# Five changes along one transformer step: the root step ahead of the weight splits, one modulation row on TensorE, shorter routing, the last index mask among the query norms, five row loads ahead of the barrier

## What is computed

```python
mod = jnp.matmul(jax.nn.silu(c), ada_w[l]) + ada_b[l]
sh1, sc1, gt1, sh2, sc2, gt2 = [m[:, None, :] for m in jnp.split(mod, 6, axis=-1)]
h = rmsnorm(x, norm1_g[l]) * (1.0 + sc1) + sh1
proj = jnp.matmul(h, w_in[l])
...
out_fox = forgetting_attention(fq, fk, fv, log_f)       # softmax with a decay
out_dsa = dsa_attention(dq, dk, dv, iq, ik, iw)         # keys chosen by an index score
...
x = x + gt1 * jnp.matmul(merged, w_out[l])
h2 = rmsnorm(x, norm2_g[l]) * (1.0 + sc2) + sh2
y = hierarchical_moe(h2, ...)
x = x + gt2 * y
```

## Time and profile before

| what | value |
|---|---|
| time of the runs, median of three | 3393.41 us (3392.14 to 3396.78) |
| time of the profiled execution | 3398.27 us |
| its span in the trace | 3396.5 us |
| TensorE busy with matmuls | 3149.5 us, 93% of the span |
| VectorE busy | 2199.0 us, 65% |
| ScalarE busy | 1329.4 us, 39% |
| GpSimd busy | 988.8 us, 29% |
| moved by the DMA engines | 446.19 MB, mean 131 GB/s |

### The profile page before, as it was taken

The page is one execution under the profiler, slowest core; times in us unless marked ns, Lnnn a source line. Parts: engine busy times, 40 slices in busy tenths (PEclk is TensorE's granted clock), DMA queues, the critical chain, the costliest instruction groups (busy, mean ns, idle before and its releaser), DMA issues. The chain is left out here.

```text
span 3396.5 us, 44909 instructions
## 1 busy us (share of the span) xinstructions
PE 3149.5 (93%) x15126; PEld 2510.4 (74%) x15126; DVE 2199.0 (65%) x2729; ACT 1329.4 (39%) x1768; POOL 988.8 (29%) x489
## 2 busy tenths in 40 slices
PE   5989989888789499999969999999999999999998
PEld 4658866565578478888857888888778888888877
DVE  7788875677544799999966776633565145245366
ACT  3345423566512388888853156201311000000142
POOL 2223322000043011111102443345234444444433
PEclk8999989899999799999989999999999999999999
DMA  6312221231151599999982122133221111111312
GB/s 241 81 50 87 75 56 55 65 120 43 44 169 69 208 377 380 378 380 383 380 314 97 50 82 91 50 121 90 83 85 44 49 49 49 50 44 49 111 38 69
DMA packets 351447, 446.19 MB, mean 131 GB/s; under 512 B 32943, under 2 KB 235613, under 8 KB 351333
## 3 DMA queue, kind: packets, MB, share of 16 engines
q1 hardware_dynamic: 336612, 410.08, 35.6%
q10 hardware_dynamic: 5360, 17.83, 1.6%
q0 software_dynamic: 9360, 16.80, 1.3%
HBM read 397.40 MB, written 58.75 MB: 134 GB/s over the span
## 5 line engine op out<-in xcount | busy, mean ns | idle before, releaser
L424 PE MATMUL acc<-Ah,whi 128*128 128x512 f32 x2208 | 875.8, 397 | 24.8 <-ACTq L1012 8.9
L397 POOL TENSOR_TENSOR whi<-wraw,one 128x1024 fp32r<-128x1024 f32 (+1 forms) x199 | 376.8, 1893 | 1717.8 <-PE acc L426 1341.3
L425 PE MATMUL acc<-Al,whi 128*128 128x512 f32 x2208 | 863.2, 391 | 0.0
L426 PE MATMUL acc<-Ah,wlo 128*128 128x512 f32 x2208 | 863.1, 391 | 0.0
L399 POOL TENSOR_TENSOR wlo<-wraw,whi 128x1024 fp32r<-128x1024 f32 (+1 forms) x199 | 517.2, 2599 | 15.6
L424 PEld LDWEIGHTS acc<-Ah,whi 128*128 128x128 f32 x2208 | 416.3, 189 | 133.9 <-issue 30.4
L425 PEld LDWEIGHTS acc<-Al,whi 128*128 128x128 f32 x2208 | 416.4, 189 | 90.3 <-issue 4.6
L426 PEld LDWEIGHTS acc<-Ah,wlo 128*128 128x128 f32 x2208 | 416.0, 188 | 88.4
L1997 DVE TENSOR_TENSOR mlo<-mraw,mhi 128x1024 fp32r<-128x1024 f32 x256 | 307.0, 1223 | 37.4 <-ACT mhi L1941 24.4
L1941 ACT ACTIVATE mhi<-mraw 128x1024 fp32r<-128x1024 f32 x256 | 268.0, 1062 | 77.9 <-PE acc L1886 50.6
L424 PE MATMUL acc<-Bh,whi 128*128 128x512 f32 x640 | 251.0, 392 | 9.5 <-POOL wlo L399 9.5
(11 more groups left out here) (565 smaller groups left out, 5020.8 us busy)
## 6 DMA issues: line engine op xcount, KB each, us to landing
mraw<-in_exp_w SPq DMA_DIRECT2D x512, 256.0 KB, 6.5
mraw<-in_exp_w SPq DMA_DIRECT2D x128, 512.0 KB, 11.5
wraw<-in_w_in SPq DMA_DIRECT2D x72, 512.0 KB, 3.8
wraw<-in_w_up SPq DMA_DIRECT2D x46, 512.0 KB, 3.8
TT<-in_ada_w SPq DMA_DIRECT2D x32, 512.0 KB, 3.8
TT<-gates SPq DMA_DIRECT2D x32, 512.0 KB, 4.5
wraw<-in_w_down SPq DMA_DIRECT2D x24, 512.0 KB, 3.9
adaraw<-in_ada_w SPq DMA_DIRECT2D x16, 512.0 KB, 9.3
```

The source lines that it names most:

```text
L397: ch(pool.tensor_tensor(hi[:, r, 0:k, 0:m], wraw[:, r, 0:k, 0:m], one[:, 0:1].unsqueeze(2).broadcast_to([P, k, m]), ALU.mult))
L424: pe.matmul(o, hi[:, hr, j, 0:m], ih[:, k0 + j, cols], start=(j == 0), stop=False)
L425: pe.matmul(o, hi[:, hr, j, 0:m], il[:, k0 + j, cols], start=False, stop=False)
L426: last = pe.matmul(o, lo[:, hr, j, 0:m], ih[:, k0 + j, cols], start=False, stop=(j == k - 1))
```

## The change

It has five parts. (1) In the head the scale rows, the two weight tiles and the shift rows are loaded ahead of the small vectors; `ada_b`, `norm1_g` and `c` come on ScalarE's queue and are turned first, the other vectors are turned inside products 0 and 1. The root step stands after the fourth scale row, and GpSimd's first splits wait for it. The eighth shift row is not summed by VectorE but multiplied on TensorE; the shift's first column has a signal of its own. (2) The mask of the last block is cut in two, which stand behind the norms of queries 5 and 6; the root of query 1 stands ahead of the swap of query 0. (3) In the routing three of eight token rows are scaled by ScalarE and shifted by GpSimd; the tile count is made by rounding; the expert of a slot by one comparison of 32 columns and a matmul; `ROWAT`'s first part is scaled by ScalarE; `IDC` is made ahead of `IDX` and `DST`. (4) Five row loads and an activation table load stand ahead of the barrier. (5) The steps of x2 signal directly.

```diff
+EARLY_VEC = 56
+DIRECT = ((), (7,))
+SUMMED = [[k for k in range(8) if k not in d] for d in DIRECT]
...
     @block.tensor
...
+        pe.wait_ge(S("ada_sum"), 1)
+        for m in range(KD):
+            last = pe.matmul(acc[0][:, 8 + m:9 + m], TT[:, 2, m * P:(m + 1) * P], one[:], start=True, stop=True)
+        last.then_inc(S("ada_cols"), 1)
+
+        shift = [acc[1][:, 0:1]] + [acc[0][:, HALF + m:HALF + m + 1] for m in range(1, KD)]
+        pe.matmul(acc[0][:, HALF:HALF + KD], ident[:], bs[:, 9, :], start=True, stop=False)
+        pe.wait_ge(S("ada_sum"), 2)
+        for m in range(KD):
+            pe.matmul(shift[m], TT[:, 3, m * P:(m + 1) * P], one[:], start=(m == 0), stop=False)
+        for k in DIRECT[1]:
+            pe.wait_ge(S(f"ada_land{k}"), 16)
+            for m in range(KD):
+                last = pe.matmul(shift[m], adaraw[1][:, k, m * P:(m + 1) * P], cact[:, 1, k:k + 1],
+                                 start=False, stop=(m in (0, KD - 1)))
+                if m in (0, KD - 1):
+                    last.then_inc(S("ada_cols"), 1)
...
-        for k in range(KD):
+        for k in SUMMED[0][:4]:
             rows(0, k)
         total, r, mean, t = (bs[:, i, :] for i in range(4))
...
+        for k in SUMMED[0][4:]:
+            rows(0, k)
+        for k in SUMMED[1][:4]:
             rows(1, k)
...
         pool.wait_ge(S("ada_sum"), 1)
+        pool.wait_ge(S("n1_root"), 2)
...
+            if j == 3:
+                pe.wait_ge(S("vec_in"), 16 * N_VEC)
+                for t, n in enumerate(VROWS):
+                    skip = 0 if t else EARLY_VEC
+                    last = pe.transpose(XX[:, t * P + skip:t * P + n], vlate[0:n - skip, t, :], ident[0:n - skip, 0:n - skip])
+                last.then_inc(S("setup"), 1)
...
             q_out(j)
+            if j == 1:
+                q_root(j)
             if 1 <= j <= 4:
                 q_swap(j - 1)
-            q_root(j)
+            if j != 1:
+                q_root(j)
...
-        for b in range(2, NB):
-            mask(b)
-        dve.sem_inc(S("searched"), 1)
+        for b in range(2, NB - 1):
+            ranked(b, E[:, 0, :], E[:, 1, :], E[:, 3, :])
+            masked(b, E[:, 0, :], E[:, 1, :], E[:, 3, :])
...
+        late = (NB - 1, E[:, 7, :], E[:, 6, :], E[:, 3, :])
+        for j in range(12):
+            q_norm(j)
             if 1 <= j <= 4:
                 q_rope(j - 1)
+            if j == 5:
+                ranked(*late)
+            if j == 6:
+                masked(*late)
+                dve.sem_inc(S("searched"), 1)
...
+        for b in BY_ACT_ROWS:
+            act.wait_ge(S("h2_turned"), TURNED.index(b) + 1)
+            ch(act.activation(hrow[:, b, :], turned[b][:], ACT.Copy, scale=root2[:, b:b + 1]))
+            act.sem_inc(acc_free[1], 1)
+            act.sem_inc(S("row_scaled"), 1)
...
+        pool.wait_ge(S("chosen"), 1)
+        for i, b in enumerate(BY_ACT_ROWS):
+            pool.wait_ge(S("row_scaled"), i + 1)
+            ch(pool.tensor_tensor(hrow[:, b, :], hrow[:, b, :], SHROW[:], ALU.add))
+            pool.sem_inc(S("row_shifted"), 1)
...
-        for j in range(T // P):
-            ch(dve.scalar_tensor_tensor(taken_by, number, float(j * P), taken_by, ALU.is_gt, ALU.add))
+        ch(dve.tensor_scalar(taken_by, Y[:, HALF + NB * N_EXP:HALF + (NB + 1) * N_EXP], 1.0 / P, 0.5 - 0.5 / P,
+                             ALU.mult, ALU.add))
+        ch(dve.tensor_scalar(taken_by, taken_by, ROUND, None, ALU.add))
+        ch(dve.tensor_scalar(taken_by, taken_by, ROUND, None, ALU.subtract))
...
         sp.wait_ge(S("experts_done"), 1)
-        for b in range(3):
+        for b in range(5):
             load_rows(sp, b)
```

More of the change, by code:

```diff
@@ L1596, in program @@
     root2, root2_t = rS[:, 8, :], rS[:, 9, :]
+    BY_ACT_ROWS, BY_DVE_ROWS, IN_XX = (1, 4, 7), (0, 2, 3, 5, 6), (2, 5)
+    turned = [(acc[0], acc[1], XX)[b % 3] for b in range(NB)]
+    TURNED = (0, 1, 2, 4, 7, 3, 5, 6)
     @block.tensor
@@ L1628, in _ @@
         last.then_inc(S("routed"), 1)
-        for b in range(2, NB):
+        for b in TURNED[5:]:
             turn_block(b)
-        pe.wait_ge(S("routed"), 3)
+        pe.wait_ge(S("routed"), 2)
+        pe.matmul(X[1][0:1, 0:SLOTS + 1], rS[:, 6, 1:2], ident[:, 0:SLOTS + 1], start=True, stop=True)\
+          .then_inc(S("routed"), 1)
+        pe.wait_ge(S("routed"), 7)
         for c in range(2 * NB):
@@ L1650, in _ @@
         act.sem_inc(S("gap_exp"), 1)
[L1651 to L1653 removed]
+        for b in (0, 2, 1, 3, 4, 5, 6, 7):
+            if b in BY_ACT_ROWS:
+                act.wait_ge(S("row_shifted"), BY_ACT_ROWS.index(b) + 1)
+            else:
+                act.wait_ge(S("h2_row"), BY_DVE_ROWS.index(b) + 1)
+            act.dma_start(h2rows[b * P:(b + 1) * P, :], hrow[:, b, :]).then_inc(S("h2_st"), 16)
+        act.wait_ge(S("routed"), 5)
+        ch(act.activation(ROWAT[:, :, 0, :], ONEAT[:], ACT.Copy, scale=rV[:]))
+        act.sem_inc(S("routed"), 1)
+    @block.gpsimd
+    def _(pool):
+        ch = chain(pool, "pool")
+        pool.wait_ge(S("chosen"), 1)
[3 more added lines that the diff above has]
+            pool.sem_inc(S("row_shifted"), 1)
     @block.vector
@@ L2096, in _ @@
         in2 = lambda c0: lambda j: W2[:, :, ds(j * P + c0, P)]
-        for b in range(3, NB):
+        for b in range(5, NB):
             load_rows(sp, b)
```

199 lines of the change are left out of this document (106 added, 93 removed).

## The result

The changed kernel takes 3364.09 us (median of four runs, 3363.52 to 3364.38) against 3394.98 for the kernel before on the same chip (3392.14 to 3396.78); the ratio is 0.9907, with a 95% interval of 0.9895 to 0.9919. The time lies in the predicted range (3345 to 3367), 8.7 us above the forecast of 3355.4. It lies outside the 3347 to 3362 that the prediction gave to the forecast itself, and where its rivals 1, 2 and 4 put the time (3363, 3363, 3360 to 3366); so the time alone doesn't say which of them holds, and the stages have to.

The account below looks back on a forecast made before the run. TensorE was taken as the bound, busy 93% of the span, so only its waits could be won. Gains 8.0 + 17 + 10 + 1.8 + 1.2 = 38.0 off 3393.4 gave 3355.4 us; range 3345 to 3367.

Parts of the forecast that it names:

- Rival 1: Query rounds stay late: the loop's excess over 12.65 (9.2 us) reaches TensorE whole, mask gives 9.5, time 3363; chance 0.13.
- rival 2: Head and routing give half: product starts at 53 (gain 4), routing gives 6, time 3363; chance 0.12.
- rival 4: Root step stays blocked or another waiter needs the last mask early: 5 to 10 falls out, 3360 to 3366; chance 0.07.
- Head: Before TensorE's first large product: reordered loads and an unblocked root step start it at 49.5 instead of 57.47; 8.0, from 6 to 11.
- The eighth row on TensorE: In the head: shift row 7 left to TensorE as eight more columns; sixteen columns end by 46.5.
- Mask: Query products: the last block's mask leaves the path ahead of query 0's norm; 17 us, from 12 to 18.7.
- the walk through the rounds: Queries 1 to 4, two accumulators: copies of queries 3 to 5 come 1 to 4 us late, only the last reaches TensorE.
- Routing: Choice to first expert product: work leaves VectorE's path or shrinks; 10 us, from 8 to 11.5.
- The rule that spoke against it: GpSimd and VectorE share a port pair, held when VectorE has two SBUF inputs; routing would give 9 instead of 10.
- Rows and x2: After the experts: fourth row lands 1.8 earlier (0 to 2.5); x2 steps release followers directly, 1.2 (0 to 2.4).
- The break at the barrier: Row loads after the experts: if they run on without this break, the fourth row lands 1.8 earlier.
- Rival 3: Slower: many short waits keep TensorE's clock at the lower level in the query products; with six, 3415; chance 0.02.

## Why the prediction was right, and where its sizes were off

**Head: right in size and for its reasons, but for one piece.** Forecast 8.0, measured 7.8 at the first product. The place of the root step is worth 6.4 and the order of the loads 3.7, each undone alone; they overlap, as their sum is over the whole. The eighth row on TensorE, which the prediction counted on, gained nothing. The prediction had 49.5 for the first product, and 49.64 came, with the sixteen columns at the lower level as it chose (they ended at 46.9, forecast 46.5).

**Mask: right in mechanism, 2.4 too high.** Forecast 17, measured 14.64. The step that failed is the walk through the rounds: "the copies of queries 3 to 5 come 1 to 4 us late, and only the last of these reaches TensorE". The copies of queries 2 to 5 came 0.8, 1.9, 3.0 and 1.2 us behind the pace, one after another, and TensorE waited for two of them (2.6 and 1.0): of the loop's excess 4.1 us reached it in all, not the 1.7 that the forecast of 17 left. Rival 1 had the mechanism, with 9.2 of excess; the truth lies between. The change put the root ahead of the swap in the first round alone, and the run with the root first in every round shows what that left: 4.0 of the 4.1 came back.

**Routing: right.** Forecast 10, measured 9.5 to the first product, and 10.0 a little later (−31.48 at the steady pace of the experts). Only the additions were undone alone; what the other pieces give (the rows that left VectorE, the count, the comparison, the order of `IDC`) was not tried one by one. That GpSimd's additions cost VectorE nothing, the row says twice: they end at 1116.74, before the count at 1117.61, and the idle ahead of that count is the same without them. The rule that spoke against it (the Trainium skill, "SBUF — State Buffer", section "SBUF: two separate sides") was not wrong but had no occasion: what ran beside the additions were token rows with an input in PSUM, at 1.28 each. The row at 37.73 that the prediction gave for that case is another one: its one input lies in SBUF and it writes to PSUM. In the head, where there was occasion, the run with the root step behind shows it three times to 0.03 us, and once the other way round: GpSimd's last split takes 2.88 for 2.35, beside a copy of VectorE that began 0.01 earlier. One of these operations (L592) has a single tensor input, in SBUF, and waited too, against the prediction's "and not where it has one"; the same section counts operations in a mode with two ports to those that contend, which the prediction left out. That may be why here, but no row tells the mode. The product of 8 columns with one input in PSUM, at 35.36 above, kept its 0.17 beside a split, as the rule has it.

**Rows and x2: right.** Forecast 1.8 and 1.2; the traces give 1.7 and 1.8, undone alone they cost 1.4 and 1.7. The break at the barrier is smaller than the prediction has it: without this part the DMA engines as a whole hardly stop there, and only the fourth row is complete late.

**The sum, and what it was taken off.** By the stages of the table the five parts gave 7.8 + 14.6 + 9.5 + 1.7 + 1.8 = 35.4, and the spans differ by 34.3. Of the 8.7 us between forecast and time, 38.0 − 35.4 = 2.6 lie in the parts, nearly all in the mask; 1.1 went in stages that the change doesn't touch; and 5.0 lie in the base: the profiled execution of before, in which the gains were read, took 3398.27, more than 25 of the 27 runs of before, while they were taken off 3393.4. The prediction called these 0.15% harmless, since they change a gain of 40 us by 0.06. That is true of a scale and false of a difference: 4.9 us is an eighth of the gain. In which stages that execution lost them, no trace tells, since there is only this one of the kernel before. Against the median of all 27 runs of before, 3395.8, the changed kernel is 32 us faster.

**The rivals.** The time fits rivals 1, 2 and 4 better than the forecast, and the range held because it took them in. The stages speak against them: rival 2 (head and routing give half) has 7.8 and 9.5 against it, rival 4 (a part falls out) five parts that all came. Rival 3 (slower, by a clock held low in the queries) fell too: the clock in 432 to 512 is 1.00, up from 0.89.

## What to carry to other kernels

Where two engines hand a buffer to and fro beside the bounding engine, write down what stands between on each queue: the issue of a transfer ahead of a short step that the other engine waits for took 2.4 us of every turn, and putting the step first in every round gave back 4.0 us over the loop. Work that can be cut from a serial stretch is worth its full time only where the next loop has slack; cut the loop as well. And take a gain of one per cent off the same execution in which it was read, or off a median of many runs, since the runs of this kernel before lie 9 us apart.
